# The last two blocks of a dense stage multiplied by token tile, and the norm behind them taken by token tile

## The reference

```python
def layer_norm(x, g, b):
    mu = jnp.mean(xf, axis=-1, keepdims=True)
    var = jnp.mean(jnp.square(xf - mu), axis=-1, keepdims=True)
    return ((xf - mu) * lax.rsqrt(var + LN_EPS) * g + b)

for l in range(DEPTH):
    mix = hgrn2_mixer(...) if l < N_A_LAYERS else diff_attention(...)   # ends in o @ w_out
    x = layer_norm(DEEPNORM_ALPHA * x + mix, ln1_g[l], ln1_b[l])
    ffn = moe_ffn(x, router_w, router_b, w_gate[l], w_up[l], w_down[l])
    x = layer_norm(DEEPNORM_ALPHA * x + ffn, ln2_g[l], ln2_b[l])
```

## Time and profile before

| | |
|---|---|
| median of 3 runs | 856.9 us (856.76 to 856.94) |
| profiled execution, its own time | 855.23 us |
| span of that execution | 853.3 us |
| mean granted TensorE clock | 0.964 of full speed |
| PE / PEld / DVE / ACT / POOL busy | 761.6 / 453.4 / 305.4 / 234.8 / 76.5 us |
| loaded from HBM | 244.57 MB |

### The profile page before, as it was taken

The page is one execution under the profiler, slowest core; times in us unless marked ns, Lnnn a source line. Parts: engine busy times, 40 slices in busy tenths (PEclk is TensorE's granted clock), DMA queues, the critical chain, the costliest instruction groups (busy, mean ns, idle before and its releaser), DMA issues.

```text
span 853.3 us, 11068 instructions
## 1 busy us (share of the span) xinstructions
PE 761.6 (89%) x4073; PEld 453.4 (53%) x4074; DVE 305.4 (36%) x532; ACT 234.8 (28%) x440; POOL 76.5 (9%) x61
## 2 busy tenths in 40 slices
PE   6997997878999989799679998889999899799982
PEld 5987885644334343353479877645344353245431
DVE  4788535561111111110674655661011111112016
ACT  3664264141102110111524656132011111012011
POOL 2023000027000000000210000026000000000000
PEclk9998998999999989999999999999999999899997
DMA  9994222649999999999954442549999999974301
GB/s 333 367 346 149 98 99 75 244 181 389 388 422 421 422 422 422 422 420 407 387 198 149 148 148 100 190 174 411 420 422 422 422 422 422 422 282 193 128 0 49
DMA packets 50967, 246.14 MB, mean 288 GB/s; under 512 B 6201, under 2 KB 6386, under 8 KB 26354
## 3 DMA queue, kind: packets, MB, share of 16 engines
q1 hardware_dynamic: 47808, 243.28, 71.6%
q10 hardware_dynamic: 3122, 2.35, 1.0%
HBM read 244.57 MB, written 1.05 MB: 288 GB/s over the span
## 4 chain that ended last, share of the span: by engine, by line
PE 67%; DMA 15%; DVE 11%; ACT 4%; issue 3%; SPq 0%; ACTq 0%; DVEq 0%
PE ps L1682 21%; DMA ring<-in_moe_w_up 14%; PE ps L1512 10%; PE ps L1694 9%; PE ps L1507 9%; PE ps L1668 3%; PE ps L1649 3%; DVE ring_lo L957 2%; PE ps L1721 2%; DVE x_lo L1361 1%; DVE stats L1018 1%; PE ps L1741 1%; PE ps L1657 1%; PE ps L1461 1%; DVE x_sb L1016 1%
## 5 line engine op out<-in xcount | busy, mean ns | idle before, releaser
L1682 PE MATMUL ps<-ring,scratch 128*64 128x512 f32 x768 | 178.0, 619 | 19.6 <-DMA ring<-in_moe_w_up 18.2
L1682 PEld LDWEIGHTS ps<-ring,scratch 128*64 128x64 f32 x768 | 60.0, 142 | 134.0 <-issue 133.1
L1694 PE MATMUL ps<-ring,scratch 128*64 128x512 f32 x512 | 113.8, 596 | 0.0
L957 DVE TENSOR_TENSOR ring_lo<-ring,w_hi 128x2048 fp32r<-128x2048 f32 x36 | 82.7, 2307 | 42.2 <-ACT w_hi L608 42.2
L608 ACT ACTIVATE w_hi<-ring 128x2048 fp32r<-128x2048 f32 x36 | 68.8, 1912 | 58.1 <-PE ps L1507 25.3
L1326 DVE TENSOR_TENSOR scratch<-ps,scratch 128x512 f32<-128x512 f32 x16 | 11.1, 692 | 175.9 <-PE ps L1682 175.8
L1694 PEld LDWEIGHTS ps<-ring,scratch 128*64 128x64 f32 x512 | 35.6, 137 | 66.6 <-issue 63.2
L567 POOL TENSOR_TENSOR scratch<-rounded,gate 128x256 f32<-128x256 f32 x16 | 13.7, 855 | 599.8 <-PE ps L1795 349.8
L1337 DVE SCALAR_TENSOR_TENSOR rounded<-ps,gslot,rounded 128x512 fp32r<-128x512 f32 x32 | 24.0, 751 | 97.0 <-ACT rounded L833 97.0
L1682 PE MATMUL ps<-spare,scratch 128*64 128x512 f32 x256 | 56.3, 592 | 0.0
L794 ACT ACTIVATE scratch<-ps,ln_col 128x256 f32<-128x256 f32 (+1 forms) x40 | 19.3, 539 | 100.3 <-PE ps L1668 95.7
(11 more groups left out here) (262 smaller groups left out, 1005.3 us busy)
## 6 DMA issues: line engine op xcount, KB each, us to landing
ring<-in_moe_w_up SPq DMA_DIRECT2D x64, 1024.0 KB, 17.4
ring<-in_moe_w_down SPq DMA_DIRECT2D x64, 1024.0 KB, 14.8
ring<-in_moe_w_gate SPq DMA_DIRECT2D x32, 1024.0 KB, 11.7
spare<-in_moe_w_gate SPq DMA_DIRECT2D x32, 1024.0 KB, 15.2
ring<-in_a_w_in SPq DMA_DIRECT2D x16, 1024.0 KB, 15.0
ring<-in_kv_w SPq DMA_DIRECT2D x8, 1024.0 KB, 14.5
ring<-in_a_w_out SPq DMA_DIRECT2D x4, 1024.0 KB, 7.8
ring<-in_b_w_q SPq DMA_DIRECT2D x4, 1024.0 KB, 14.5
```

The source lines that it names most:

```text
L957: V.tensor_tensor(ring_lo[:, piece_slot(i), :, :], ring[:, piece_slot(i), :, :], w_hi[:, i % HI, :, :].bitcast(F32), ALU.subtract).then_in ...
L1682: last = mm(ps[half, bank, :], xe[:, HALF_K * part + k, own], weight(odd, matrix, part, e)[:, k, :], start=part == 0 and k == 0, stop=part ...
L1694: last = mm(ps[half, bank, :], hT[:, 2 * part + k, half], weight(odd, DOWN, part, e)[:, 2 * k + cols, :], start=part == 0 and k == 0, stop ...
```

## The change

TensorE no longer multiplies AO0's and then AO1's second half (in layer 1 BO0's and BO1's). A new function takes the two pieces together: for token tile 0 the three passes, each over both blocks, then the same for tile 1. So both halves of tile 0's rows are complete after 24 of the 48 matmuls. VectorE and ScalarE take the norm in the same manner, tile by tile, each with its own variance, root and scale. ScalarE normalises all of tile 0 and the second half of tile 1's features; VectorE normalises only the first half of tile 1's. `x_done[1]` therefore counts two steps per such norm, and the waits on it, on `ln_stat` and on the roots are renumbered. A place of the two last pieces counts as read when all 48 matmuls are done. The norms behind the experts stay as they are. The diff, without the renumbered calls:

```diff
+LAST = (AO0, AO1, BO0, BO1)
...
         def multiplied(i):
             n, part = PIECES[i]
+            if part and n in LAST:
+                return proj_ready, 2 * (n - n % 2) + 4
             return (proj_ready, 2 * n + 2) if part else (half_done, n + 1)
...
+            def normalise_by_token(i, first_root):
+
+                for t in range(TT):
+                    root(first_root + t, lambda r: rs[:, r, t:t + 1])
+                    act.wait_ge(ln_stat, 3 * (i // 2) + t + 1)
+                    halves = slice(t, 2)
+                    nc.scalar.activation(tiles(xn[:, t, :], HALF_K)[:, halves], by_tile(x[:, t, :], HALF_K)[:, halves],
+                                         ACT.Identity, scale=rs[:, 2, t:t + 1], bias=rs[:, 4, t:t + 1]
+                                         ).then_inc(x_done[t], 1)
...
-            root(2, ln_values)
-            normalise(0)
+            normalise_by_token(0, 2)
...
-            def residual_projection(n):
-                for t in range(TT):
-                    dve.wait_ge(proj_ready, 2 * n + t + 1)
-                    residual(t, n % 2, ps[:, 4 + 2 * (n % 2) + t, :])
+            def projections_normed(n0, rt_call):
+
+                def sums(t, half):
+                    dve.wait_ge(proj_ready, 2 * n0 + 2 * t + half + 1)
+                    last = residual(t, half, ps[:, 4 + 2 * half + t, :])
+                    if half:
+                        step(last)
+
+                def moments(t):
+                    step(V.bn_aggr(mv[:, t, :], stats[:, t, :, :].rearrange("p a b -> p (a b)")))
+                    V.tensor_scalar(rs[:, 0, t:t + 1], mv[:, t, 1:2], LN_EPS, None, ALU.add).then_inc(var_ready, 1)
+
+                def scales(t):
+                    step(rstd(rt_call + t, lambda r: rs[:, r, t:t + 1]))
+                    V.scalar_tensor_tensor(rs[:, 4, t:t + 1], mv[:, t, 0:1], -1.0, rs[:, 2, t:t + 1], ALU.mult, ALU.mult
+                                           ).then_inc(ln_stat, 1)
+
+                sums(0, 0)
+                sums(0, 1)
+                moments(0)
+                sums(1, 0)
+                scales(0)
+                sums(1, 1)
+                moments(1)
+                scales(1)
+                V.tensor_scalar(tiles(xn[:, 1, :], HALF_K)[:, 0:1], by_tile(x[:, 1, :], HALF_K)[:, 0:1],
+                                mv[:, 1, 0:1], rs[:, 2, 1:2], ALU.subtract, ALU.mult).then_inc(x_done[1], 1)
...
-            residual_projection(AO0)
-            residual_projection(AO1)
-            layer_norm(0, 2)
+            projections_normed(AO0, 2)
...
+            def last_pieces(i):
+
+                n0 = PIECES[i][0]
+                assert PIECES[i:i + 2] == [(n0, 1), (n0 + 1, 1)]
+                call = 1 if n0 == AO0 else 3
+                for t in range(TT):
+                    for number, half in ((0, 0), (0, 1), (1, 0), (1, 1), (2, 0), (2, 1)):
+                        m = i + half
+                        if t == 0 and number == 0:
+                            pe.wait_ge(hi_ready, m + 1)
+                            pe.wait_ge(x_hi_ready, 2 * call + 2)
+                            pe.wait_ge(x_hi_dve, {1: 4, 3: 6}[call])
+                        if t == 0 and number == 1:
+                            pe.wait_ge(x_lo_ready, 2 * call + 2)
+                        if t == 0 and number == 2:
+                            pe.wait_ge(lo_ready, m + 1)
+                        w = ring_lo[:, piece_slot(m), :, :] if number == 2 else w_hi[:, m % HI, :, :]
+                        xs = y_lo if number == 1 else y_hi
+                        for k in range(HALF_K):
+                            last = mm(ps[:, 4 + 2 * half + t, :], xs[:, HALF_K + k, t * P:(t + 1) * P], w[:, k, :],
+                                      start=False, stop=number == 2 and k == HALF_K - 1, skip_group_check=True)
+                        if number == 2:
+                            last.then_inc(proj_ready, 1)
...
-            piece(18)
-            piece(19)
+            last_pieces(18)
```

More of the change, by code:

```diff
@@ L548, in affine @@
                     pool.wait_ge(x_done[0], i + 1)
-                    pool.wait_ge(x_done[1], i + 1)
+                    pool.wait_ge(x_done[1], 3 * (i // 2) + 2)
                     for t in range(TT):
@@ L798, in moe @@
                 act.wait_ge(x_done[0], 2 * layer + 1)
-                act.wait_ge(x_done[1], 2 * layer + 1)
+                act.wait_ge(x_done[1], 3 * layer + 2)
                 nc.scalar.activation(xr_hi.rearrange("p t n -> p (t n)"), xn.rearrange("p t n -> p (t n)"),
@@ L856, in _ @@
             moe(0)
-            root(3, ln_values)
+            root(4, ln_values)
             normalise(1)
@@ L924, in _ @@
             heads_out(5)
-            root(4, half_values(0))
+            root(5, half_values(0))
             probabilities(7)
@@ L935, in _ @@
             heads_out(7)
-            root(5, half_values(1))
+            root(6, half_values(1))
             mixed_high(4, 2, lambda k: pcol[:, 24:25])
-            root(6, ln_values)
-            normalise(2)
+            normalise_by_token(2, 7)
             transposed(5, 2)
@@ L942, in _ @@
             moe(1)
-            root(7, ln_values)
+            root(9, ln_values)
         @block.vector
@@ L1005, in layer_norm @@
                                        ).then_inc(ln_stat, 1)
[L1006 to L1009, removed]
+                V.tensor_scalar(x[:, 0, :], x[:, 0, :], mv[:, 0, 0:1], rs[:, 2, 0:1], ALU.subtract, ALU.mult
+                                ).then_inc(x_done[0], 1)
             added = [0]
@@ L1353, in _ @@
             moe(0)
-            layer_norm(1, 3)
+            layer_norm(1, 4)
             transposed(3, 1)
@@ L1441, in _ @@
             low(34)
[L1442 removed]
+            rms_of_sums(6, 1, 8)
             scaled(1)
@@ L1446, in _ @@
             dve.wait_ge(x_affine, 2)
-            residual_projection(BO0)
-            residual_projection(BO1)
-            layer_norm(2, 6)
+            projections_normed(BO0, 7)
             transposed(5, 2)
@@ L1452, in _ @@
             moe(1)
-            layer_norm(3, 7, final=True)
+            layer_norm(3, 9, final=True)
         @block.tensor
@@ L1461, in turn, with turn_all @@
                 return nc.tensor.transpose(ps[:, k // 2, first:first + P], src[:, t, k * P:(k + 1) * P], ident[:, :])
-            def turn_all(src, ready, value):
+            def turn_all(src, ready, values):
                 for t in range(TT):
-                    pe.wait_ge(ready[t], value)
+                    pe.wait_ge(ready[t], values[t])
                     for k in range(KT):
@@ L1820, in _ @@
                 nothing(0)
-            turn_all(xn, x_done, 1)
+            turn_all(xn, x_done, (1, 2))
             moe(0)
@@ L1826, in _ @@
                 nothing(BANK_A)
-            turn_all(x, x_done, 2)
+            turn_all(x, x_done, (2, 3))
             def attention_scores(h):
@@ L1894, in _ @@
             turn_half(1, 4)
-            piece(34)
-            piece(35)
+            last_pieces(34)
             for _ in range(18):
                 nothing(0)
-            turn_all(xn, x_done, 3)
+            turn_all(xn, x_done, (3, 5))
             moe(1)
```

12 lines of the change are left out of this document (4 added, 8 removed).

## The result

The changed kernel takes 859.9 us (median of 20 runs, 856.7 to 863.15), the kernel before 855.77 us in the same rounds (20 runs, 853.58 to 857.98). The ratio is 1.005, 95% interval 1.0039 to 1.0061: 4.1 us slower. The forecast was 857.4 and its range ended at 859.0; it was wrong. It stood on a median of 856.9 from 3 runs of the kernel before; against that it forecast 0.5 us of loss. What happened is the mechanism of rival C, which had 4 in 100.

A forecast was written before the change was run, and what follows sets the result against it. The chain through tile 1's normalisation to the gate matmuls, which starts the expert stage's DMA stream, was taken as the bound; 0.23 us in each of two layers, 0.46, gave 855.7 profiled, 857.4 with the median's 1.7; range 855.6 to 859.0.

The forecast's parts named there:

- rival C: TensorE idling around tile 1's transposes drops its clock, doubling transposes, router and fold: 2.2 us per layer, 861.8; 4 in 100.
- The norm's path: VectorE and ScalarE chain up to tile 1's normalised rows: x_done[1] at 171.79 instead of 171.56, 0.23 us late per layer.
- the matmul order: TensorE's 48 reordered matmuls in the dense stage: VectorE starts its last stretch at 164.55 either way, no cost.
- chunk 10's load: DMA queue: this load goes out later, the stream ends 2.5 us later inside a pause lasting until 190.67; cost 0.
- the tight wait of layer 1: TensorE's wait for the second block's low part, moved from matmul 41 to 21: met with 1.0 us to spare.
- the step that put the clock at nothing in the sum: TensorE's clock left out of the forecast sum; a fall would need the longer pause to stretch by some 1 us.
- PEclk stays at 1.00 in 170:177: Sign to check in layer 0's profile: TensorE's granted clock stays full from 170 to 177 us.
- again while the columns are copied: TensorE's second idle stretch, after the one from about 170.3 to 171.8 between the tiles' transposes; no size given.
- Rival B: Tile 0's scale is done in VectorE's wait before 164.55; last normalisation ends 1.14 us early: 854.6; 2 in 100.
- Rival A: ScalarE alone on x_sb is fast, 1.24 and 0.62 us for its two normalisations: 855.1; 8 in 100.
- the half-wide instruction: ScalarE's normalisation of half of tile 1's features: 1.21 us forecast, between bounds of 0.62 and 2.25.
- passed on one to one: Expert stage's DMA stream starts when the compute chain reaches the gate matmuls, so the chain's gain or loss carries over fully.

The follow-up runs named there:

- e4_peorder: The kernel before with only the matmul half of the change (order, additions, later chunk 10 load) and the old norm: 855.31 us, ratio 1.0001.
- e11_rfill: The changed kernel with seven matmuls on zeros ahead of the router matmuls, the pause between the tiles' transposes left in: 856.27 us, ratio 1.0002.
- e1_fill: The changed kernel with six more matmuls on zeros between the transposes of tile 0 and tile 1: 855.97 us, ratio 1.0004.
- e5_fewer: The changed kernel with 12 instead of 18 matmuls on zeros behind the fold matmuls: 862.94 us, ratio 1.0071 to the kernel before.
- e3_early: The changed kernel with tile 0's scale finished before the third addition instead of behind it: 853.69 us, ratio 0.9967 to the kernel before.
- e10_fill3: The changed kernel with three matmuls on zeros between the two tiles' transposes: 859.99 us, ratio 1.0054 to the kernel before.
- r1_after: The changed kernel run once more, unaltered, for a second profiled execution: 860.35 us, ratio 1.0051 to the kernel before.
- r2_before: The kernel before run once more, unaltered, for a second profiled execution: 856.15 us, ratio 1.0005.
- e6: e3_early with seven more matmuls on zeros ahead of the router matmuls: 853.29 us, ratio 0.9965 to the kernel before.
- e8: e6 with VectorE also taking a fourth of ScalarE's half of tile 1's normalisation: 853.55 us, ratio 0.9968 to the kernel before.
- e2_pause: The kernel before with 12 instead of 18 matmuls on zeros ahead of the attention and mixer norms' transposes: 862.37 us, ratio 1.0072.

## Why the prediction was wrong

The read of the waits and of the queue order was right. The norm's path grew by 0.12 us in layer 0 (forecast 0.23), tile 1's transposes started as forecast, the matmul order and chunk 10's load cost nothing (e4_peorder), and the tight wait of layer 1 held: the 48 matmuls ran without a stop.

What failed is the step that put the clock at nothing in the sum and gave it 4 in 100. In the prediction's words, "PEclk stays at 1.00 in 170:177". I compared the new pause of 1.5 us with single pauses: 1.11 us, after which the clock stayed, and 2.46, after which it fell, and concluded that the new one would have to stretch by 1 us. The measured pause was 1.52 us and did not stretch, and the clock fell to 0.50. Both comparisons left out the neighbours. The 2.46 us were themselves the second of two pauses, which the rows of before show:

```profile
418.40 1.96 PE L1461 MATMUL ps<-ident,x_sb 128*128 128x128 f32 x16 [2.58 <-DVE x_sb L1009]
```

Behind the first, of 2.58 us, the clock stayed at 1.00 until 423; it fell behind the second. And for the stage itself I had said that TensorE idles "again while the columns are copied". The change splits one stretch of work, tile 0's and tile 1's transposes back to back, and so puts one pause from before it in between. e11_rfill shows that filling the second pause alone, and e1_fill that filling the first alone, takes the loss away.

The size of rival C was off in its parts. It doubled the transposes (0.45), which stayed fast, the router and the fold: 2.2 us per layer. Measured in the profiled pair: router and fold matmuls 0.87 and 0.41 more. Then a term that I had not priced, since the fillers were counted as nothing: at the lower clock the 18 fillers behind the fold last longer than the wait that they fill, and the rank matmuls stand behind them in TensorE's queue. The rank came 6.42 us behind the start of the fold matmuls instead of 4.80 (the fold's 0.41 is in this). e5_fewer confirms it: with 12 fillers 1.2 us of this came back in layer 0. Together 2.57 and 2.30 us per layer, near the 2.2 plus 0.23 of the rival, by other terms; that the sizes agree is luck.

Rival B's mechanism was right and is what e3_early makes: it forecast the last normalisation's end 1.14 us earlier than before. Measured from the first filler in the first profiled executions, tile 0's transposes alone started at +5.17 before; tile 1's started 171.62 less 165.28, 6.34, and 5.30 in e3_early, 1.04 earlier. Rival A fell: ScalarE took 2.24 us. It was not quite alone on x_sb (VectorE's L1023 and L1025 were there for 1.3 us of it), but the half-wide instruction settles it: 0.69 us of its 1.30 lie behind the end of VectorE's share at 170.59, more than the 0.62 that the rival gave for the whole. So the strided read costs by itself.

Open: what the clock's fall goes by exactly. e10_fill3 differs between its two layers and e3_early too, with the same pauses in each. Open too is the spread behind the gate, where the prediction said that what the chain loses is "passed on one to one": between the two profiled pairs these two stretches were 0.7 to 1.4 us longer each with the changed norm (362.05 and 285.24 against 361.33 and 283.83; in r1_after and r2_before 363.13 and 285.11 against 362.07 and 284.22). Part of it goes with falls near 205 us, in some executions and not in others; that this follows from the change is not shown. In layer 1, among executions without a fall near 591, the three with the gate at +23.6 (changed, r1_after, e10_fill3) took 285.1 to 285.2 us from there to the end, the eight with the gate at +21.3 to +21.5 took 283.8 to 284.7, and the three with the gate at +20.0 to +20.3 (e3, e6, e8) took 284.8 to 285.1. On the means the late gate cost 0.9 us more than its lateness, and of an early one the single traces show little at the end; the gain of e3 and e6 rests on their medians.

## What to carry to other kernels

When a change moves work between pauses of TensorE, look at the neighbouring pauses and at the work between them instead of weighing each pause by itself: two of 1.5 and 1.7 us with 1.1 us of work between cost here what neither cost alone, while 1.8 and 1.7 with 2.3 between cost nothing. This gives no rule that predicts the clock, so where it matters, fill the pause and measure. Fillers that stand in the queue ahead of real work were free here only at the full clock (18 took 4.04 us, at the lower one 5.7); count them at the lower one. And where work is taken tile by tile so that it overlaps, the small instructions of the first tile must stand in the program ahead of the wait for the second, or the overlap isn't there: that one line made the difference between 0.5% slower (ratio 1.005) and 0.3% faster (0.9967).

## What was not expected of the hardware

A pause of 2.54 us at 205 us left the clock alone in one execution of the changed kernel, and one of 2.53 was followed by the lower one in e5_fewer, with the same instructions around it. Ahead of the same matmuls 2.67 us left it alone in before (203.44) and did not in r1_after (204.65). Six fewer matmuls on zeros ahead of a norm (e2_pause) made the kernel 6.5 us slower, more than the whole change.
